# Two mixer layers: the order of small steps around queries, keys and the memory's transposes

## The reference, cut to what matters

```
h = rms_norm(x, norm_g[l]);  proj = h @ w_in[l]
q_a, k_a, v_a, q_h, f_h, i_h, q_m, z = split(proj)      # 512 columns each, z has 3 * 512
qa, ka = partial_rope(rms_norm(q_a)), partial_rope(rms_norm(k_a))   # 8 heads of 64
o_a = softmax_causal(qa @ ka.T) @ v_a
log_f = logaddexp(log(lb), log1p(-lb) + log_sigmoid(f_h));  kf = (1 - lb) * sigmoid(-f_h)
o_h = rms_norm(recurrence(silu(q_h), log_f, kf, i_h))    # 4 heads of 128
km, vm = split(rms_norm(mem) @ w_mem_kv[l]);  qm, km = rms_norm per head
o_m = softmax(qm @ km.T) @ vm                            # 4 heads of 128
x = x + (concat(o_a, o_h, o_m) * silu(z)) @ w_out[l]
```

## Time and profile before

| | us |
|---|---|
| median of 3 runs (lowest, highest) | 1517.25 (1516.98, 1519.36) |
| profiled execution, its own time | 1516.82 |
| span of that execution in the profile | 1515.0 |
| TensorE busy | 1448.2 |
| DVE busy | 956.1 |
| ACT busy | 693.9 |

### The profile page before, as it was taken

The page is one execution under the profiler, slowest core; times in us unless marked ns, Lnnn a source line. Parts: engine busy times, 40 slices in busy tenths (PEclk is TensorE's granted clock), DMA queues, the critical chain, the costliest instruction groups (busy, mean ns, idle before and its releaser), DMA issues.

```text
span 1515.0 us, 19971 instructions
## 1 busy us (share of the span) xinstructions
PE 1448.2 (96%) x8234; PEld 1217.2 (80%) x8234; DVE 956.1 (63%) x1161; ACT 693.9 (46%) x971; POOL 52.8 (3%) x41
## 2 busy tenths in 40 slices
PE   5999899999899999999998999989999999899997
PEld 4888788888787988886647999869888855499986
DVE  7688677698676479654326656457795534465653
ACT  4754575754574475431124434346743320443432
POOL 0002000002000001000000000000100000000000
PEclk8999999999999999999999999999999999999999
DMA  8544235544333554333444655455533334355653
GB/s 266 166 142 146 84 131 167 168 138 141 96 125 118 197 193 140 112 112 111 139 135 144 187 176 180 153 186 174 175 112 112 111 111 167 111 179 183 189 172 113
DMA packets 138985, 225.79 MB, mean 149 GB/s; under 512 B 7888, under 2 KB 54288, under 8 KB 138768
## 3 DMA queue, kind: packets, MB, share of 16 engines
q1 hardware_dynamic: 133456, 221.60, 44.6%
q10 hardware_dynamic: 5440, 2.93, 0.6%
HBM read 223.46 MB, written 1.05 MB: 148 GB/s over the span
## 4 chain that ended last, share of the span: by engine, by line
PE 87%; ACT 4%; DVE 4%; issue 2%; ACTq 1%; POOL 1%; DMA 1%; POOLq 0%; DVEq 0%
PE gp L561 43%; PE gp L552 21%; PE gp L534 6%; PE mp L828 5%; PE gp L611 3%; PE mp L516 3%; PE mp L670 2%; DVE wt_rest L1375 1%; PE mp L724 1%; DVE arena L1369 1%; POOL rs_out L2033 1%; ACT first_hi L1014 1%; PE mp L791 1%; ACT arena L1245 1%; PE mp L821 0%
## 5 line engine op out<-in xcount | busy, mean ns | idle before, releaser
L1375 DVE TENSOR_TENSOR wt_rest<-wt,wt_hi 128x1024 fp32r<-128x1024 f32 x140 | 164.9, 1221 | 70.6 <-ACT wt_hi L1014 70.5
L1014 ACT ACTIVATE wt_hi<-wt 128x1024 fp32r<-128x1024 f32 x140 | 140.2, 1051 | 115.3 <-DMA wt<-in_ffn_down 58.9
L1375 DVE TENSOR_TENSOR wt_rest<-wt,mix_hi 128x1024 fp32r<-128x1024 f32 x112 | 132.6, 1222 | 55.8 <-ACT mix_hi L1014 55.0
L552 PE MATMUL gp<-hT_hi,wt_hi 128*128 128x256 f32 x576 | 163.3, 284 | 0.0
L552 PE MATMUL gp<-hT_hi,wt_rest 128*128 128x256 f32 x576 | 163.0, 283 | 0.0
L552 PE MATMUL gp<-hT_rest,wt_hi 128*128 128x256 f32 x576 | 163.0, 283 | 0.0
L561 PE MATMUL gp<-wt_rest,mix_hT_hi 128*128 128x512 f32 x384 | 154.3, 402 | 0.0
L561 PE MATMUL gp<-mix_hi,mix_hT_hi 128*128 128x512 f32 x352 | 143.3, 407 | 8.6 <-DVE arena L1795 5.6
L1014 ACT ACTIVATE mix_hi<-wt 128x1024 fp32r<-128x1024 f32 x112 | 114.7, 1060 | 79.2 <-PE gp L561 29.8
L1375 DVE TENSOR_TENSOR wt_rest<-wt,first_hi 128x1024 fp32r<-128x1024 f32 x104 | 122.5, 1220 | 28.1 <-ACT first_hi L1014 27.8
L561 PE MATMUL gp<-mix_hi,mix_hT_rest 128*128 128x512 f32 x352 | 138.5, 394 | 0.0
(11 more groups left out here) (297 smaller groups left out, 3091.7 us busy)
## 6 DMA issues: line engine op xcount, KB each, us to landing
wt<-in_w_in SPq DMA_DIRECT2D x100, 1024.0 KB, 5.0
wt<-in_ffn_gate SPq DMA_DIRECT2D x44, 512.0 KB, 4.0
wt<-in_ffn_up SPq DMA_DIRECT2D x44, 512.0 KB, 5.0
wt<-in_w_out SPq DMA_DIRECT2D x20, 1024.0 KB, 5.0
wt<-in_ffn_down SPq DMA_DIRECT2D x20, 1024.0 KB, 5.0
wt<-in_w_mem_kv SPq DMA_DIRECT2D x8, 1024.0 KB, 5.1
wt<-in_w_branch_pool SPq DMA_DIRECT2D x4, 1024.0 KB, 5.0
wt<-in_w_branch_ret SPq DMA_DIRECT2D x4, 1024.0 KB, 5.0
```

Source lines behind the costliest of these rows:

```text
L552: last = nc.tensor.matmul(o, a[:, k, P * c:P * c + P], b[:, :, k0 + k, :], start=(k0 + k == 0 and c % 2 == 0 and i == 0), stop=(k0 + k == ...
L1014: nc.scalar.activation(rounded_part(u)[:, k:k + nk, :], wt[:, u % SLOTS, k:k + nk, :], ACT.Copy)\
L1375: return nc.vector.tensor_tensor(o, i0, i1, ALU.subtract)
```

## The change

In A0 and A1 TensorE's steps `mpt0` to `mpt3` come ahead of `qaT` and `kaT`, and ACT copies their results first, ahead of the move of Z2. ACT's sigmoid of Z2 goes from behind that move to behind the copies of queries and keys. On DVE the remainders of unit 19 (the second of Z2) go ahead of the four maxima of the memory's scores. In A1 alone, a small operation on the lower bound and two waits move up to the norm of the memory's keys, and the maximum over `etmp` and the product with `ks` move behind the product of QH and behind the remainders of unit 9. No instruction is added or removed.

```
@@ ORDER_1
-    + ["hg8_1", "qmT0", "qmT1"] + [ms0..ms3] + ["qaT0", "qaT1", "kaT0", "kaT1"] + [mpt0..mpt3] \
+    + ["hg8_1", "qmT0", "qmT1"] + [ms0..ms3] + [mpt0..mpt3] + ["qaT0", "qaT1", "kaT0", "kaT1"] \
@@ tensor
                 split_units(s("Z2"), 1)
+                mem_transposes()
                 for src, n in (("QA", "qaT"), ("KA", "kaT")):
                     for t in range(TT):
                         transposes(...)
-                mem_transposes()
@@ scalar
                 round_until(20)
+                for h in range(NH):
+                    evacuate(f"mpt{h}", mprT[:, h], bank(s(f"mpt{h}"), 4, P))
                 move(s("Z2"))
-                gate_sigmoid(2)
                 ... copies of qaT and kaT ...
-                for h in range(NH):
-                    evacuate(f"mpt{h}", mprT[:, h], bank(s(f"mpt{h}"), 4, P))
+                gate_sigmoid(2)
                 round_until(21)
@@ vector
                 mul(km, km, over(given(asked), 8, P)).then_inc(sig("km_normed"), 1)
+                if l == 1:
+                    dve.wait_ge(sig("lb_ln"), 1)
+                    v(nc.vector.scalar_tensor_tensor(lbs[:, 0:8], dd, 0.0, small[:, 496:504], ALU.min, ALU.subtract))
+                    dve.wait_ge(sig("lb_sig"), 1)
...
                 if l > 0:
-                    dve.wait_ge(sig("lb_ln"), 1)
-                    v(nc.vector.scalar_tensor_tensor(lbs[:, 0:8], dd, 0.0, small[:, 496:504], ALU.min, ALU.subtract))
-                    dve.wait_ge(sig("lb_sig"), 1)
                     v(add(etmp, ...)); v(sub(dtmp, ...)); absolute(dtmp, dtmp)
                 rests_until(8)
-                if l > 0:
-                    v(nc.vector.tensor_tensor(etmp, etmp, lbs[:, 0:4]..., ALU.max))
-                    v(mul(ks, ks, lbs[:, 8:12]...))
                 dve.wait_ge(sig("hg_q_sig"), l + 1)
                 mul(qs_b, group_banks(s("QH")), qs_b).then_inc(group_read[...], 1)
                 rests_until(9)
+                if l > 0:
+                    v(nc.vector.tensor_tensor(etmp, etmp, lbs[:, 0:4]..., ALU.max))
+                    v(mul(ks, ks, lbs[:, 8:12]...))
...
+                rests_until(19)
                 for h in range(NH):
                     ... maximum of ms{h}, then_inc(sig("mem_max"), 1) ...
-                rests_until(19)
```

More of the change, by code:

```diff
@@ L96 @@
 ORDER_1 = [f"xT{i}" for i in range(4)] + ["kmT0", "kmT1"] + [f"hg{n}_{t}" for n in range(8) for t in range(2)] \
-    + ["hg8_1", "qmT0", "qmT1"] + [f"ms{h}" for h in range(4)] + ["qaT0", "qaT1", "kaT0", "kaT1"] + [f"mpt{h}" for h in range(4)] \
+    + ["hg8_1", "qmT0", "qmT1"] + [f"ms{h}" for h in range(4)] + [f"mpt{h}" for h in range(4)] + ["qaT0", "qaT1", "kaT0", "kaT1"] \
     + ["om0", "om1", "hgo0", "hgo1"] + [f"sc{h}" for h in range(4)] + ["yT4", "yT5"] + [f"sc{h}" for h in range(4, 8)] + ["yT2", "yT3"] \
@@ L1570, in _ @@
                 rests_until(8)
-                if l > 0:
-                    v(nc.vector.tensor_tensor(etmp, etmp, lbs[:, 0:4][:, :, None].to_broadcast([P, NH, S]), ALU.max))
-                    v(mul(ks, ks, lbs[:, 8:12][:, :, None].to_broadcast([P, NH, S])))
                 dve.wait_ge(sig("hg_q_sig"), l + 1)
@@ L1578, in _ @@
                 rests_until(9)
+                if l > 0:
+                    v(nc.vector.tensor_tensor(etmp, etmp, lbs[:, 0:4][:, :, None].to_broadcast([P, NH, S]), ALU.max))
+                    v(mul(ks, ks, lbs[:, 8:12][:, :, None].to_broadcast([P, NH, S])))
                 if l > 0:
```

## The result

The changed kernel takes 1502.1 us (median of 4 runs, 1501.89 to 1503.4), the kernel before 1517.37 in the same comparison: a ratio of 0.9895 with a 95% interval of 0.9881 to 0.991. Forecast were 1501.0 us and 1498 to 1507.

What follows compares the result with a forecast made beforehand. TensorE, busy 96%, was taken as the bound, so only its losses in A0 and A1 could be won: 7.8 + 6.3 + 2.1 = 16.2 us off 1516.82, plus 0.43 for the median, gives 1501.0 us; range 1498 to 1507.

Steps and rivals of the forecast that it cites:

- What bounds it, and comparing stretches: TensorE, busy 96%, sets the pace; memory's scores to Z1's second unit needs 24.44 us without waits, against 32.26 and 30.73.
- 7.8 and 6.3: Gains in us taken for the stretches of A0 and A1, from the memory's scores to Z1's second unit.
- Edit 1: Z2's second unit: remainders ahead of the four maxima let TensorE start at 152.12; the rotation ends at 159.0.
- Edit 2: Memory's transposes before queries and keys, sigmoid last: eight steps run through to 161.28; the late sigmoid costs nothing.
- 3.6 us of cover: Behind Z2's late sigmoid: remainders of Z1's second unit done by 170.6, wanted at 173.1, so no cost.
- some 3: Sign to look for: DVE idle before the Z2 gate product some 3 us longer.
- Edit 3: A1's early part, DVE reordered: 2.1 us gained, with new waits of about 1.0 on the scan and 0.6 at unit 10.
- Rival 1: TensorE's clock falls in the new order, 1.5 us in each of A0 and A1: 1504.1 us; chance 0.15.
- (2): A new wait, on the rotation or bank reuse at kaT1, costs each layer 1.0 us: 1503; chance 0.12.
- (3): Half the gain isn't there: stretch bound by ACT, or later stages wait for loads; about 1509 us; chance 0.05.
- (4): Sigmoid behind the copies delays DVE, costing once it ends after 170.5; at 180 in both layers, 1520 us; chance 0.03.
- The sum: 7.8 + 6.3 + 2.1 = 16.2 us off the profiled 1516.82, plus 0.43 for the median: 1501.0 us.

Runs made afterwards that it cites:

- order_back: Changed kernel with the memory's transposes behind queries and keys again on TensorE and ACT, sigmoid still last: 1505.21 us, ratio 0.9921.
- order_alone: Kernel before with only the new order of the memory's transposes on TensorE and ACT: 1506.19 us, ratio 0.9933.
- no_edit1: Changed kernel with the remainders of unit 19 behind the four maxima again: 1507.61 us, ratio 0.993.

## Why the prediction was right

**What bounds it, and comparing stretches.** Right. The work without waits was put at 24.44 us and takes 24.29 in both layers. The 7.8 and 6.3 were 7.97 and 6.44. The waits alone would have given two thirds of the 7.97. The prediction names 4.8 us of them in A0 and says that the half us for the rotated queries is in no list; it is, as a third row of the list from 60 to 270 us:

```profile
PE mp L516 <- DVE arena L1372: 0.5, 1, 0.5
```

With it the waits are 5.3 us. The other 2.7 are the fall of the clock (1.5) and slow first instructions.

**Edit 1.** Right: the prediction lets TensorE start the unit at 152.12 where it was 154.41, 2.3 us, and taking the edit back costs 2.39. The maxima started at 150.63 (forecast 150.56) and the rotation ended at 159.07 (159.0).

**Edit 2.** Right in the sum, and its order is the part that pays (`order_back`, `order_alone`). The late sigmoid costs nothing, as said, but the reason given was too wide: the step "3.6 us of cover" counted only the remainders of Z1's second unit. DVE had 0.42 us of idle time at its next meeting with TensorE, and the real room is about 0.6 us. The sentence that from 173.1 on the next events hang on TensorE was true only by that little. DVE's idle time before the gate product grew from 0.80 to 5.86 us, 5.1 more and not "some 3": the prediction counted the later sigmoid, but not that its own edit 1 brings DVE there 1.6 us earlier.

**Edit 3.** Right: 2.1 us forecast, 13.85 - 12.00 = 1.85 in E and 0.13 to the start of it. The new wait on the scan is 1.00 (1.0), the one behind it 0.37 (0.6). But 1.54 of these 1.85 us are the fall of the clock that doesn't come any more, and only 0.31 the reordering (`order_alone`). The prediction took the fall of the profiled execution as a cost that is always there. With the same stops it came in two profiles of three, so that this term fits is in part luck.

**Rival 1, the clock.** Its price of 1.5 us was right: 1.47 in `no_edit1`, 28.17 - 26.68 = 1.49 in `order_alone`. It did not come in the changed kernel, and in the profiles of all kernels with the new order no fall began in the 32 transposes. The first profile, 157.79 to 161.40 us, at a granted 1.00:

```profile
157.79:161.40 3.61, 3.61 (x34) 3.61 (x33) 3.48 (x5) 2.98 (x6) 0.00 (x0) 1.00 0.62 180
```

The Trainium skill ("TensorE: Matmul & The Clock Gate", Part 4: PE-mode transpose) says that transposes don't count as activity for the clock as matmuls do. The rows of the new order don't bear that out. One row of the kernel before leaves it open: in A0 its clock fell at about 167 us, within the last 12 transposes, but behind two stops of 2.1 and 0.6 us; the same transposes and stops in A1 had no fall.

**Rivals 2, 3 and 4.** No wait took the place in the stretches (2); ACT was not their bound (3); the sigmoid was not late enough (4), though the point from which it costs, 167.2 + 0.6 = 167.8, lay some 3 us nearer than the 170.5 us given.

**The sum.** 16.2 us forecast, 16.33 at the end of the last stretch, 15.27 in the medians. The term that was missing is that of clock falls in untouched stages, which was priced at the low end of the range only, as one fall that doesn't come. Here one of before (477 us) didn't come, two grew longer, and one came at 1009 us where there was none. In the stretches the forecast was right by its mechanism. That the median lies as near as 1.1 us is in part luck, as one program varies by more than that in the rest of the kernel.

## What to carry to other kernels

Where an engine is busy 96% of the time, don't add its waits: take the stretch from one anchor to the next and subtract the work at its undisturbed pace. That also catches slow first instructions and falls of the clock, which were a third of the gain in A0. A fall in the one profile that you start from may not be there in the next, so price the stretch with it and without it.

When work is moved behind other work, follow every later meeting of the delayed engine with the bound one, not only the first; the second one here had a sixth of the room. And where a chain on a second engine (here DVE's up to the scan) has nothing taken away, reordering it only moves the wait: look for idle time ahead of the chain to put a member of it into.

## What the runs showed of the hardware that was not expected

A short stop of TensorE can bring a fall of its clock to the 1.2 GHz level in one execution and not in another, for identical programs: 460 to 468 us had a granted 1.00 and 0.79 in two profiles of one kernel. The same stop also had a fall behind it in one layer and none in the other: at unit 19, with the new order, 2.1 us of stop were followed by a fall in A0 and not in A1 (`no_edit1`), and in A1 and not in A0 (`order_alone`). In the kernel before neither layer has one directly behind it. A fall costs 1.5 us in these stages. Executions of the changed kernel and of the one with the sigmoid back lie between 1499.1 and 1503.9 us, so a difference of up to about 3 us (an estimate) can't be told from nothing by a few runs, while the trace tells a tenth of a us up to the first fall.
